# ScalarE builds the diagonal of a row's weight, and the pairs of row slots are written out

## What is computed

```
q = (xt @ w_q).reshape(T, PEER_HEADS, 2, PEER_HALF)            # T = 256, 8 heads
sc = jnp.einsum('thcd,hckd->thck', q, sub_keys)
s1, i1 = lax.top_k(sc[:, :, 0], K)                             # K = 16 of 128 keys
s2, i2 = lax.top_k(sc[:, :, 1], K)
cand = (s1[..., :, None] + s2[..., None, :]).reshape(T, PEER_HEADS, K * K)
top_s, top_pos = lax.top_k(cand, K)
gate = jax.nn.softmax(top_s, axis=-1)
...
hid = jax.nn.gelu(jnp.einsum('tkd,td->tk', u[ib], xb), approximate=False)
return jnp.einsum('tk,tkd->td', (gb * hid).astype(xb.dtype), v[ib])
```

## Time and profile before

| what | value |
|---|---|
| time, median of 3 runs | 2476.85 us (2476.78 to 2477.72) |
| span of the profiled execution | 2470.5 us |
| the two PEER parts in the trace | about 805 to 1480 us and 1752 to 2428 us |
| busy over the span | PE 86%, DVE 70%, ACT 32%, POOL 24% |
| DMA over the span | 294 GB/s |

### The profile page before, as it was taken

The page is one execution under the profiler, slowest core; times in us unless marked ns, Lnnn a source line. Parts: engine busy times, 40 slices in busy tenths (PEclk is TensorE's granted clock), DMA queues, the critical chain, the costliest instruction groups (busy, mean ns, idle before and its releaser), DMA issues.

```text
span 2470.5 us, 28939 instructions
## 1 busy us (share of the span) xinstructions
PE 2128.4 (86%) x9222; PEld 1383.0 (56%) x9222; DVE 1718.6 (70%) x3650; ACT 780.9 (32%) x1437; POOL 589.4 (24%) x520
## 2 busy tenths in 40 slices
PE   7999899999999887778877778999897877877877
PEld 7999789989777552223322237877653222322324
DVE  5455665558565778788787876646777877878785
ACT  4334643346664221111111125344321111111113
POOL 0000000000000434443444430000344434444440
PEclk9999999999999999999999999999899999999999
DMA  6555335545224999999999994544799999999994
GB/s 249 181 185 172 118 120 184 179 168 177 103 79 169 391 352 388 420 421 420 405 421 420 420 420 165 188 153 148 300 370 368 420 421 420 401 421 420 421 420 165
DMA packets 101175, 726.46 MB, mean 294 GB/s; under 512 B 11616, under 2 KB 11744, under 8 KB 13280
## 3 DMA queue, kind: packets, MB, share of 16 engines
q0 software_dynamic: 74016, 539.00, 53.3%
q1 hardware_dynamic: 25200, 181.41, 21.0%
q10 hardware_dynamic: 1872, 4.88, 0.6%
HBM read 724.21 MB, written 1.05 MB: 294 GB/s over the span
## 4 chain that ended last, share of the span: by engine, by line
PE 48%; DVE 17%; issue 14%; DMA 14%; ACT 4%; POOL 2%; DVEq 1%; POOLq 0%; ACTq 0%
PE bank L1623 48%; DMA arena<-in_uv,expert 14%; DVE arena L1536 2%; DVE lw_rounded L1054 2%; POOL arena L573 2%; DVE arena L1561 1%; ACT w_hi L625 1%; DVE arena L1513 1%; DVE arena L1509 1%; DVE sel_i L1515 1%; DVE arena L1478 1%; DVE top_i L1487 1%; ACT xn L663 1%; DVE arena L1492 1%; DVE top_i L1476 1%
## 5 line engine op out<-in xcount | busy, mean ns | idle before, releaser
L1623 PE MATMUL bank<-arena 128*128 128x512 f32 (+2 forms) x2472 | 1062.1, 568 | 249.0 <-DVE arena L1536 245.3
L1623 PEld LDWEIGHTS bank<-arena 128*128 128x128 f32 (+1 forms) x2472 | 427.1, 193 | 864.8 <-DVE arena L1536 544.4
L573 POOL DMA_INDIRECT arena<-in_uv,expert x512 | 578.7, 1130 | 1209.6 <-PE bank L1623 667.8
L1561 DVE SCALAR_TENSOR_TENSOR arena<-arena,xn 128x1024 f32<-128x1024 f32 x512 | 626.6, 1224 | 189.3 <-DMA arena<-in_uv,expert 180.2
L1054 DVE TENSOR_TENSOR lw_rounded<-lw,w_hi 128x2048 fp32r<-128x2048 f32 x169 | 389.1, 2306 | 235.9 <-ACT w_hi L625 232.6
L969 ACT ACTIVATE act_h<-hid 128x1 f32<-128x1 f32 x512 | 102.6, 202 | 1004.1 <-DVE arena L1561 996.9
L1623 PE MATMUL bank<-xT_hi,w_hi 128*128 128x256 f32 x1352 | 388.2, 287 | 26.8 <-DVE lw_rounded L1054 18.5
L625 ACT ACTIVATE w_hi<-lw 128x2048 fp32r<-128x2048 f32 x169 | 323.0, 1917 | 278.5 <-PE bank L1623 253.2
L1623 PE MATMUL bank<-xT_lo,w_hi 128*128 128x256 f32 x1352 | 384.6, 284 | 0.0
L1623 PE MATMUL bank<-xT_hi,lw_rounded 128*128 128x256 f32 x1352 | 384.5, 284 | 0.0
L1623 PEld LDWEIGHTS bank<-xT_hi,w_hi 128*128 128x128 f32 x1352 | 260.7, 193 | 37.7 <-DVE lw_rounded L1054 29.3
(11 more groups left out here) (201 smaller groups left out, 1488.4 us busy)
## 6 DMA issues: line engine op xcount, KB each, us to landing
lw<-in_units SPq DMA_DIRECT2D x171, 1024.0 KB, 4.8
arena<-in_uv,expert POOLq DMA_INDIRECT x512
wide<-in_wide POOLq DMA_DIRECT2D x2, 1024.0 KB, 10.6
gain<-in_gains ACTq DMA_DIRECT2D x4, 512.0 KB, 7.6
h<-in_x SPq DMA_DIRECT2D x2, 512.0 KB, 6.3
arena<-in_ret_consts ACTq DMA_DIRECT2D x1, 1024.0 KB, 5.9
out<-xn SPq DMA_DIRECT2D x2, 512.0 KB, 2.6
consts<-in_consts ACTq DMA_DIRECT2D x1, 592.5 KB, 5.9
```

Of the source, the lines that this page charges most:

```text
L573: nc.gpsimd.indirect_dma_start(out=rows_uv[:, slot, :], out_offset=None, in_=table, in_offset=bass.IndirectOffsetOnAxis(ap=expert[par][:, ...
L1561: V.scalar_tensor_tensor(rows_uv[:, slot, 0:D], rows_uv[:, slot, 0:D], 1.0, xn[:, tile, :], ALU.mult, ALU.mult, accum_out=hid[par][:, k:k ...
L1623: return nc.tensor.matmul(o, lhsT, rhs, start=start, stop=stop, **more)
```

## The change

`spread` moves from DVE to ACT and is called directly behind the gelu of its own step. ACT has no instruction that multiplies by two columns in one go, so there are two: the first multiplies the gelu column by the weight column (128x1), the second multiplies the identity by the result (128x128). Each waits for ACT's own instruction before it. The wait for a free `diag` buffer moves along, and at the first step of a row ACT also waits until `weigh` of that row is done. DVE loses the diagonal and its two waits, and keeps everything else in its order. `peer_rows` writes all eight pairs out on the three engines that use it, so the waits there are against constants.

```diff
         def peer_rows(eng, tile, rows):
-            first = tile * PEER_HEADS
-            if tile == 0:
-                rows(first, 0, LATE_HEADS)
-                first += 2
-            with eng.Fori(0, ((tile + 1) * PEER_HEADS - first) // 2) as i:
-                rows(first, i, {})
+            for first in range(tile * PEER_HEADS, (tile + 1) * PEER_HEADS, 2):
+                rows(first, 0, LATE_HEADS if first == 0 else {})
...
+                def spread(s, row, par, k):
+                    if k == 0:
+                        act.wait_ge(top_order, row * CHOICE + (layer * (ROWS + 1) * CHOICE + CHOICE))
+                    act.wait_ge(gelu_done, s + (layer * ROWS * TOPK + 1))
+                    nc.scalar.activation(act_h[par][:, k:k + 1], act_h[par][:, k:k + 1], ACT.Identity,
+                                         scale=weight[par][:, k:k + 1]).then_inc(coef_ready, 1)
+                    act.wait_ge(slot_free, s + (layer * ROWS * TOPK + SLOTS * (layer + 1) - DIAGS + 1))
+                    act.wait_ge(coef_ready, s + (layer * ROWS * TOPK + 1))
+                    nc.scalar.activation(diag[:, k % DIAGS, :], ident, ACT.Identity, scale=act_h[par][:, k:k + 1]).then_inc(diag_ready, 1)
...
                             nc.scalar.activation(act_h[par][:, k:k + 1], hid[par][:, k:k + 1], ACT.Gelu).then_inc(gelu_done, 1)
+                            spread(i * (2 * TOPK) + ((row + par) * TOPK + k), i * 2 + (row + par), par, k)
...
-                def spread(s, par, k):
-                    dve.wait_ge(gelu_done, s + (layer * ROWS * TOPK + 1))
-                    dve.wait_ge(slot_free, s + (layer * ROWS * TOPK + SLOTS * (layer + 1) - DIAGS + 1))
-                    V.tensor_scalar(diag[:, k % DIAGS, :], ident, act_h[par][:, k:k + 1], weight[par][:, k:k + 1],
-                                    ALU.mult, ALU.mult).then_inc(diag_ready, 1)
...
-                                spread(i * (2 * TOPK) + (row * TOPK + k - 1), par, k - 1)
...
-                        spread(i * (2 * TOPK) + (row * TOPK + TOPK - 1), par, TOPK - 1)
```

More of the change, by code:

```diff
@@ L91 @@
 DIAGS = 4
+CHOICE = 28
 EARLY_HEADS = 3
@@ L502, in build @@
         gelu_done = sem("gelu_done")
+        coef_ready = sem("coef_ready")
         diag_ready = sem("diag_ready")
@@ L1456, in peer @@
                 dve.wait_ge(score_act, 9 * layer + 1)
-                CHOICE = 28
                 def pick(row, par):
```

## The result

The changed kernel takes 2484.53 us (median), the kernel before in the same rounds 2476.85: a ratio of 1.0029, 95% interval 1.0018 to 1.0039. The forecast was 2464 us with a range from 2452 to 2473: a gain was forecast, and a loss of 7.7 us measured. The profiled execution took 2480.66 us with a span of 2478.9, against 2470.5 before: 8.4 us more. Each of the executions listed for these two kernels stands 1.8 us above its own span; the 6.35 us of the forecast are these 1.8 and 4.5 us by which the profiled execution of the kernel before was faster than the median.

What follows compares the result with a forecast made beforehand. The prediction took each PEER step to last as long as its 1 MB gather at 420 GB/s. Terms -9.8 - 4.0 + 0 + 0.5 + 0.5 = -12.8 us gave a 2457.7 us span, plus 6.35: 2464 us, range 2452 to 2473.

Steps and rivals of the forecast that it cites:

- I take 0.5 us, between 0 and 2.8.: Written-out code on the three engines: fetching up to 1.16 MB through DMA was put at 0.5 us lost.
- Rival 3: Gathers' DMA engines: fetching the new straight code stalls where nothing hides it, 2550 us; chance 0.07.
- Term A: Late heads, lacking 20.3 us of DMA time: nothing comes back, between 4 us lost and 12 gained.
- Term B: Steps behind the last late head: DVE no longer stops at the diagonal, all 9.8 us gained, at least 5.
- Term C: Steps behind the change of tile: 4.0 of the lacking 5.0 us gained, between 1 and 5.
- The step's chain: One PEER step: from the dot's start to the ready diagonal, 2.19 us after the change instead of 4.00.
- rival 4: ACT's tables: Identity not in gelu's table, so every step loads two, 2950 us; chance 0.03.
- rival 2: Late heads: DVE arrives with dots done, half or more of their lacking time also returns, 2452 us; chance 0.14.
- A rule on engine time: Diagonal on ACT: 664 ns against DVE's 349; if engine time counted, the change would cost 161 us.

## Why the prediction was wrong, by its own steps

**"I take 0.5 us, between 0 and 2.8."** This step failed first. I priced the new code by its bytes spread over all DMA engines. The runs price it at 12.6 us (2484.53 less 2471.93), all but 1.0 of it VectorE's. A packet goes to one DMA engine, and each of VectorE's holds the same one back by 0.98 us where the gathers keep all sixteen busy; each dot waits for the slowest. The bytes are nothing: 22 more packets of 8 KB on q14, 0.18 MB, of which 13 are VectorE's. My sentence "the loop edges lie in stretches at 420 GB/s, so they gain nothing" had the sign of the danger turned round: those are the very stretches where a fetch is paid.

**Rival 3** had the right cause and side and the wrong place. I looked for "idle time that nothing in the profile ends" on an engine; there is none, it is idle time ended by a DMA. At 1 us for each extra q14 packet (22, less 13.8) its own sum gives 2485 us, where the 87 came from doubling all packets. That this meets the measured 2484.5 is luck: only 13 of the 22 cost anything, and 7 us are the clock's. The forecast gave the rival a chance of 0.07. The Trainium skill, "Runtime: NRT & Kernel Launch", section "Instruction fetch mechanics", says that straight code is fetched ahead and that crossing a block boundary is mostly hidden. For VectorE the trace agrees, for it never stalls for its code; it was wrong to let the rival fall by that, since the fetch is paid in the gathers (2492.84 us written out against 2477.97 looped).

**Term A** was sized by hand at nothing, within -12 to +4 of change. The hand sum put the products of the five heads between 1.1 us earlier and 0.3 later; in the profile, against step 0 of the layer, the first head's start 1.1 earlier, as forecast, but the fourth's 0.5 later and the fifth's 2.8. The 0.7 us for each step between scores and rounding were nearly right (0.82). What was missing is what a longer stand of PE does: 2.14 us instead of 0.91, and the clock falls to 1.2 GHz on the very products that everything waits for, 1.5 us for each of six. With PE kept busy the change gains 7.1 us. The row that could have warned stood in the earlier trace rows: PE waits behind ACT's chain, and the clock column of every late-head stretch stood at 1.00 with waits of 0.9 to 1.5 us. I read the column as settled. The trace of before has the price elsewhere: the 48 products that begin at 806.74, behind a stand of 4.39 us, take 7.40 us, with the granted clock at 0.5 for 3.4 us. The range did not carry the term's own lower bound either: it took 1.5 of the 4 us that A could lose. With all 4 it would have ended near 2476, still under the result.

**Term B** (-9.8) held in kind and was sized too large: with code and clock mended it lacks 2.6 of 9.8 us, so 7.2 came back by the stretches, and 5.6 by the steps (32 to 48 of both layers against before). In the changed kernel itself steps 32 to 48 gain 0.8 and 1.5 us, and A had lost 1.9 and 2.2 by step 32.

**Term C** (-4.0) failed in the changed kernel: PE stood on the projection at the half clock, 1150 to 1200 us lacks 2.4 + 0.5 where it lacked 2.3. Looped and with the busy products, 1150 to 1200 and 2100 to 2140 lack 0.7 in all, of 5.0: the size was right, 4.3.

**The step's chain** was forecast at 2.19 us and is 2.29; the table loads did not multiply (rival 4).

Put together, the forecast of 2464 us is what the change does without the two missed causes: looped, and with PE kept busy, it takes 2467.1. The other 17.4 us are 7.1 of the clock and 10.3 of the straight code, or 12.6 of the code and 4.8 of the clock when the code is mended first. That 2467 lies so near to 2464 says little: B brought less than forecast, and the two causes were not in the sum. Beyond that, rival 2 (A comes back, 2452 us) needs the earlier rounding: 2457.5.

**A rule on engine time.** ScalarE takes 295 + 402 = 697 ns for what VectorE did in 349. The Trainium skill's page "ScalarE: Activation LUTs" ("Rules for kernel authors") would have the multiplication on VectorE, and by engine time the trace agrees. The move still gains 6 us in the looped version: what counted was the queue that the work stood in.

## What to carry to other kernels

Where gathers keep every DMA engine busy, write out each engine's loop by itself before writing out all of them: here only VectorE's straight code cost anything. A fetch is not paid in bytes or in a stall but by one DMA engine that falls behind, seen as a jump between landings at an unchanged rate. Look at which of a gather's sixteen signals each fetch moves: fetches that hit the same one add up, others hide behind the latest. When work is moved to another engine, look at what stands in that queue ahead of a wait of TensorE's; a wait grown from 0.91 to 2.14 us cost the clock on top here. And move first what does not depend on the thing it stands behind: taking the rounding from behind the scores was worth 9.6 us in the looped change and 4.8 in the kernel before, the diagonal 6.

## What the runs showed of the hardware that was not expected

- An 8 KB instruction packet of VectorE's takes 0.325 us, and the gather packet that begins where it ends takes 0.968 us instead of 0.313. Together they hold one of the sixteen DMA engines back by 0.98 us, and the lag stays until the gathers pause. Behind ScalarE's 8 KB packets the gather packet takes 0.687 us (0.68 us of lag), behind TensorE's 16 KB packets of 1.02 to 1.11 us it takes 0.76 to 0.86 (about 1.55). Why a packet behind a fetch takes longer is open.
- VectorE's fetches move one and the same signal of the sixteen, ScalarE's another one, and TensorE's a different one each time. So ten more 16 KB packets cost 1.3 us in all (ratio 1.0007, interval from 0.9998), and 16 more of VectorE's 8 KB packets 14.9.
- The granted clock fell to 0.5 within 1.3 us of the products' start behind stands of 2.14 and 2.79 us in the changed kernel and of 1.97 us in the looped one with the earlier rounding. It did not behind stands of 0.91, 1.17 and 1.47 us there in the kernel before, nor of 1.71 us in the last kernel named.
